# Reordered small passes of a recurrent layer: whole exponentials for the decay, keys on VectorE, memory scores between substitution steps

## The reference

```python
w = -softplus(-(w0 + tanh(dw) @ w_up)) - 0.5
a = sigmoid(a0 + da @ a_up)
kk = hs(k * k_k)                                     # 12 heads of 64
kk = kk * rsqrt(max(sum(kk * kk, -1), 1e-24))
k = hs(k * (1.0 + (a - 1.0) * k_a))
decay = exp(-exp(w))
# for each token:
sa = einsum('bhij,bhj->bhi', state, kk_t)
state = state * w_t - sa * (kk_t * a_t) + v_t * k_t
out = einsum('bhij,bhj->bhi', state, r_t)
```

## Time and profile before

| | |
|---|---|
| median of three runs | 1571.17 us |
| the profiled execution, its own time | 1572.52 us |
| its span in the trace | 1571.1 us |
| TensorE busy | 1482.2 us, 94% |
| TensorE weight load busy | 1339.4 us, 85% |
| VectorE busy | 899.7 us, 57% |
| ScalarE busy | 727.0 us, 46% |
| GpSimd busy | 96.9 us, 6% |
| mean granted TensorE clock | 0.978 of full |

### The profile page before, as it was taken

How to read it: one execution, slowest core, us unless ns; L and a number is a source line. 1 busy time by engine, 2 the same in 40 slices (tenths; PEclk the granted TensorE clock), 3 DMA queues, 4 the chain that set the end, 5 groups by cost and what they waited for, 6 DMA issues and landing times.

```text
span 1571.1 us, 23220 instructions
## 1 busy us (share of the span) xinstructions
PE 1482.2 (94%) x9817; PEld 1339.4 (85%) x9817; DVE 899.7 (57%) x1157; ACT 727.0 (46%) x1021; POOL 96.9 (6%) x122
## 2 busy tenths in 40 slices
PE   7899899999999999995999999999999998899997
PEld 5787887998789987894987899879998797789986
DVE  4765646555465556577446655566555665565554
ACT  4654544444454443875212544425444366454441
POOL 3001000000000000000211000000000112300000
PEclk9999999999999999987999999999999999999999
DMA  8634626665575663641002666547656462265651
GB/s 285 221 113 148 242 76 192 181 192 190 162 226 168 202 195 121 195 125 64 1 14 81 205 184 190 192 142 234 187 183 201 147 215 81 68 214 175 199 191 67
DMA packets 121607, 254.06 MB, mean 162 GB/s; under 512 B 8040, under 2 KB 33824, under 8 KB 121248
## 3 DMA queue, kind: packets, MB, share of 16 engines
q1 hardware_dynamic: 117200, 237.07, 48.3%
q0 software_dynamic: 4304, 15.51, 3.1%
HBM read 251.50 MB, written 1.05 MB: 161 GB/s over the span
## 4 chain that ended last, share of the span: by engine, by line
PE 81%; DVE 10%; ACT 5%; issue 2%; DMA 2%; POOL 0%; ACTq 0%; DVEq 0%; POOLq 0%
PE ps L1671 79%; DVE wl L1034 2%; DVE xres L1048 2%; DMA raw<-in_w_in 1%; ACT wh L511 1%; DVE st L1104 1%; ACT bsa L521 1%; PE ps L1763 1%; DVE xl L1042 1%; PE ps L2101 1%; PE ps L1784 0%; DVE st L1051 0%; DMA gb<-in_g_mix_pre 0%; DVE bsw L1042 0%; ACT junk L521 0%
## 5 line engine op out<-in xcount | busy, mean ns | idle before, releaser
L1034 DVE TENSOR_TENSOR wl<-raw,wh 128x1024 fp32r<-128x1024 f32 x448 | 545.6, 1226 | 471.9 <-ACT wh L511 470.0
L511 ACT ACTIVATE wh<-raw 128x1024 fp32r<-128x1024 f32 x448 | 469.8, 1058 | 481.5 <-PE ps L1671 436.9
L1671 PE MATMUL ps<-xh,wh 128*128 128x256 f32 x1792 | 505.7, 282 | 3.0 <-DVE xl L1042 3.0
L1671 PE MATMUL ps<-xl,wh 128*128 128x256 f32 x1792 | 503.1, 281 | 0.0
L1671 PE MATMUL ps<-xh,wl 128*128 128x256 f32 x1792 | 502.9, 281 | 0.0
L1671 PEld LDWEIGHTS ps<-xh,wh 128*128 128x128 f32 x1792 | 339.8, 190 | 6.1 <-DVE xl L1042 3.6
L1671 PEld LDWEIGHTS ps<-xl,wh 128*128 128x128 f32 x1792 | 339.8, 190 | 0.3
L1671 PEld LDWEIGHTS ps<-xh,wl 128*128 128x128 f32 x1792 | 339.6, 189 | 0.0
L1671 PE MATMUL ps<-wh,fhh 128*128 128x512 f32 x440 | 171.2, 389 | 0.0
L1671 PE MATMUL ps<-wl,fhh 128*128 128x512 f32 x440 | 171.2, 389 | 0.0
L1671 PE MATMUL ps<-wh,fhl 128*128 128x512 f32 x440 | 171.2, 389 | 0.0
(11 more groups left out here) (338 smaller groups left out, 1491.1 us busy)
## 6 DMA issues: line engine op xcount, KB each, us to landing
raw<-in_ffn_w_gate SPq DMA_DIRECT2D x88, 512.0 KB, 3.9
raw<-in_ffn_w_up SPq DMA_DIRECT2D x88, 512.0 KB, 4.0
raw<-in_ffn_w_down SPq DMA_DIRECT2D x88, 512.0 KB, 4.2
raw<-in_w_out SPq DMA_DIRECT2D x24, 512.0 KB, 3.5
raw<-in_w_gate SPq DMA_DIRECT2D x22, 512.0 KB, 3.8
raw<-in_w_up SPq DMA_DIRECT2D x22, 512.0 KB, 4.0
raw<-in_w_down SPq DMA_DIRECT2D x22, 512.0 KB, 4.2
raw<-in_rwkv_w_in SPq DMA_DIRECT2D x22, 512.0 KB, 4.1
```

What stands on the lines that cost most here:

```text
L511: act.activation(wh[:, i % NH, :], raw[:, i % NR, :], ACT.Copy).then_inc(act_done.new(("hi", i)), 1)
L1034: dve.tensor_tensor(wl[:, i % NH, :], raw[:, i % NR, :], wh[:, i % NH, :].bitcast(F32), ALU.subtract).then_inc(dve_done.new(("lo", i)), 1)
L1671: return pe.matmul(o, l, r, start=start, stop=stop, skip_group_check=True)
```

## The change

Five things change, all between the projection units of the recurrent layer.

1. The exponentials of the decay. Before: 12 ScalarE instructions of 128 columns for `e1` and 12 for `e3`, each with its own bias column. Now VectorE subtracts the value of token 63 from all sums in one wide subtraction (`lr`, written where the decay will stand), and ScalarE does `e3` and `e1` as one instruction each, 128x1536, in that order. Both stand behind the rounding of unit 14, and `e3` no longer stands behind the squares.
2. `kk` moves from ScalarE (six copies) to VectorE (one wide product); `kk2` writes to `LD` instead of `BV`. On VectorE `kk`, `ka`, `nb`, `kp` and `b` move ahead of `n2`, and `k1` behind it. `ze`, the small exponential, moves behind the square root `i24`.
3. `xi0`, which zeroes the off-diagonal part of the inverse, and `rk` move later; `by_row` moves ahead of `z_in(12)` and `z_in(14)` on ScalarE, and the first two gram masks on VectorE ahead of the `wl` of unit 21.
4. On VectorE the substitution steps are no longer followed by the scores: `wl` of unit 26 and `one_x(0)`, `one_x(1)` stand between step 7 and step 8. ScalarE does the exponentials of heads 0 and 1 ahead of `xi`, which stood behind it before.
5. The division by the sum is done by ScalarE (`shares`, four copies with a scale column for each pair of heads) instead of VectorE.

```diff
@@ ScalarE @@
             z_in(10, 0)
-            act.wait_ge(*dve_done.by("63"))
-            for m in range(12):
-                fn(decay[:, m, 1:P + 1], twelve(w1)[:, m, :], ACT.Exp, "e1", m, scale=DEC, bias=down63[:, m:m + 1])
-            fn(decay[:, :, 0], down63, ACT.Exp, "e0")
-            act.wait_ge(*dve_done.by("zt", 10))
-            for c in range(6):
-                copy(KK[:, c, :], Kk[:, c, :], "kk", c, scale=V("rwkv_k_k_2", c))
-            act.wait_ge(*act_done.by("kk", 5))
-            fn(BV[:, :, :], KK[:, :, :], ACT.Square, "kk2")
+            hi_to(after("rw", 0, 0))
+            act.wait_ge(*dve_done.by("zsc"))
+            fn(decay[:, :, 0], twelve(w1)[:, :, 63], ACT.Exp, "e0", scale=-DEC)
+            act.wait_ge(*act_done.by("e0"))
+            fn(twelve(w1), decay[:, :, 1:P + 1], ACT.Exp, "e3", scale=-DEC)
+            fn(decay[:, :, 1:P + 1], decay[:, :, 1:P + 1], ACT.Exp, "e1", scale=DEC)
+            act.wait_ge(*dve_done.by("kk"))
+            fn(LD, KK[:, :, :], ACT.Square, "kk2")
             hi_to(after("rw", 0, 1))
-            act.wait_ge(*act_done.by("e1", 11))
-            for m in range(12):
-                fn(twelve(w1)[:, m, :], twelve(w1)[:, m, :], ACT.Exp, "e3", m, scale=-DEC, bias=up63[:, m:m + 1])
-            fn(zsc[:, :], zsc[:, :], ACT.Exp, "ze", scale=DEC)
             hi_to(after("rw", 0, 2))
             act.wait_ge(*dve_done.by("n2"))
             fn(i24[:, :], i24[:, :], ACT.Sqrt, "i24")
+            fn(zsc[:, :], zsc[:, :], ACT.Exp, "ze", scale=DEC)
...
@@ ScalarE, after the projection @@
-            act.wait_ge(*dve_done.by("inverse_by_row"))
-            for i in range(4):
-                copy(XI[strip[i], :, strip[i]], inverse_by_row[strip[i], :].rearrange("p (m i) -> p m i", i=32)[:, 0:24, :], "xi", i)
+            def shares(h):
+                act.wait_ge(*dve_done.by("rc", "r", h))
+                for tb in range(2):
+                    copy(rpb[:, h, tb, :], rpb[:, h, tb, :], "p", "r", h, tb, scale=mem_st(h, 6)[:, tb:tb + 1])
+
             one("r", 0)
             one("r", 1)
...
+            shares(0)
+            shares(1)
+            act.wait_ge(*dve_done.by("inverse_by_row"))
+            for i in range(4):
+                copy(XI[strip[i], :, strip[i]], inverse_by_row[strip[i], :].rearrange("p (m i) -> p m i", i=32)[:, 0:24, :], "xi", i)
             one("r", 2)
             one("r", 3)
+            shares(2)
+            shares(3)
@@ VectorE @@
-            ts(down63, twelve(w1)[:, :, 63], -DEC, None, ALU.mult, ALU.bypass, "down63")
-            ts(up63, twelve(w1)[:, :, 63], DEC, None, ALU.mult, ALU.bypass, "63")
+            tt(decay[:, :, 1:P + 1], twelve(w1), twelve(w1)[:, :, 63:64].to_broadcast([P, 12, P]), ALU.subtract, "lr")
...
+            tt(KK[:, :, :], Kk[:, :, :], VB("rwkv_k_k_2"), ALU.mult, "kk")
+            lo_to(after("rw", 0, 0))
```

More of the change, by code:

```diff
@@ L830, in act_program @@
             z_in(4, 0)
[L831 to L832 removed]
+            hi_to(after("rw", 1536, 0))
             act.wait_ge(*dve_done.by("zt", 4))
@@ L835, in act_program @@
                 copy(BV[:, c, :], Rr[:, c, :], "rk", c, scale=V("rwkv_r_k_2", c))
+            hi_to(after("rw", 1536, 1))
+            act.wait_ge(*pe_done.by("norms"))
+            copy(XI, C(K_ONE, P).unsqueeze(1).to_broadcast([P, 24, P]), "xi0", scale=0.0)
+            hi_to(after("rw", 1536, 2))
+            act.wait_ge(*dve_done.by("gram", 2, 1))
+            for i in range(4):
+                copy(by_row[strip[i], 0:C7].rearrange("p (m t) -> p m t", t=32), AP[strip[i], :, strip[i]], "by_row", i)
             hi_to(after("rw", 1536, 3))
@@ L1501, in dve_program @@
                 substitute(j)
+            lo_to(after("rw", 1536, 3))
+            z_in(12)
+            z_in(14)
             lo_to(after("rw", 2048, 0))
-            for j in range(5, 10):
+            for j in range(5, 8):
                 substitute(j)
@@ L1513, in dve_program @@
             one_x(1)
+            for j in range(8, 15):
+                substitute(j)
+            one_p(0)
+            one_p(1)
+            dve.wait_ge(*dve_done.by("inverse", 14))
+            dve.transpose(inverse_by_row.rearrange("p (m i) -> p i m", i=32), inverse).then_inc(dve_done.new(("inverse_by_row",)), 1)
+            one_x(2)
+            one_x(3)
             dve.wait_ge(*dve_done.by("k1"))
```

62 lines of the change are left out of this document (20 added, 42 removed).

## The result

| | kernel before | changed kernel |
|---|---|---|
| median of 13 runs (lowest to highest) | 1570.82 us (1567.62 to 1573.98) | 1561.36 us (1555.46 to 1566.93) |
| ratio, 95% interval | | 0.9941 [0.9927, 0.9955] |
| profiled execution, span | 1572.52, 1571.1 us | 1565.0, 1563.7 us |
| mean granted clock | 0.978 | 0.983 |

The changed kernel is 9.5 us faster, by the interval 7.1 to 11.5 us. The forecast was 1563.5 us with 1560.5 to 1567.5 around it. The two profiled executions lie 7.5 us apart.

The account below looks back on a forecast made before the run. TensorE, busy 81% of the span, was taken as the bound, so only its waits in the stage counted. Gains of 1.6 and 6.1 us sum to 7.7, taking the median from 1571.2 to 1563.5 us, range 1560.5 to 1567.5.

Parts of the forecast that it names:

- Wide exponentials at 1.4 us: ScalarE, decay: each of the two wide exponentials takes 1.4 us, like the square over the same 1536 columns.
- Rival A: ScalarE, decay: the wide exponentials cost double, 2.96 us each; sum 4.9 us, time 1566.3 us; chance 0.06.
- The squares at 665.4 us: ScalarE, ahead of the norms: both wide exponentials end at 665.4 us, then the squares run until 667.0 us.
- `n2` at 674.5 us: VectorE, ahead of the norms' spreading: six wide passes and smaller work come first, giving 674.5 us against 673.8 before.
- The table load: ScalarE, at the norms: the square root's load runs ahead of its wait; a 1.28 us load follows, no drain counted.
- First term: From the sums to the spreading of the norms: a gain of 1.6 us, from -1.2 to 2.1.
- Second transpose at the same time: VectorE, at the substitution: it starts at 723.8 us as before, the earlier start being taken by 5.7 us of moved work.
- Second term: From gram to the transposes of the shares: a gain of 6.1 us, bounds 4.5 and 7.0.
- B: VectorE waits inside the substitution for the first scores; with a landing of 7.5 us, time 1567.3 us; chance with D 0.12.
- C: The substitution is held by the weight transfer; at a landing of 16 us, 4.7 us slower, 1576 us; chance 0.04.
- D: Gram to shares: scores were bound by the substitution's end, not the order; gain 2.9, time 1568.3 us; chance with B 0.12.
- The shares on ScalarE, 0.2 us: Ahead of ScalarE's copy of the first transposes: four shares, 1.65 us, mostly hidden by TensorE's transposes; 0.2 us cost.

Follow-up runs that it names:

- narrow24: The changed kernel with its two wide exponentials cut into 24 of 128 columns; median 1564.30 us, ratio 0.9959 to the kernel before.
- p1_only: The kernel before with only the edits to decay, keys and norms; gram, substitution and scores as before; median 1568.43 us, ratio 0.9988 to the kernel before.
- p2_only: The kernel before with only the edits to substitution, scores and shares; median 1564.07 us, ratio 0.9957 to the kernel before.
- xi0_late: The changed kernel with ScalarE's fill of xi0 moved behind the wait for the last gram masks, directly ahead of by_row; median 1564.37 us, ratio 0.9961 to the kernel before.
- scores_late: The changed kernel with maxima, exponentials and reciprocals of heads 0 and 1 back behind the second transpose and xi; median 1571.30 us, ratio 1.0009 to the kernel before.
- again: The changed kernel itself, unedited, run for a second trace; median 1562.25 us, ratio 0.994 to the kernel before.
- xi_late: The changed kernel with heads 2 and 3's maxima ahead of the last two substitution steps and xi's copies among the others; median 1562.81 us, ratio 0.9947 to before.
- copies_first: The changed kernel with heads 2 and 3's maxima earlier, and their shares and the first share copies ahead of xi; median 1561.95 us, ratio 0.995 to before.

## Why the prediction was right, step by step

- **Wide exponentials at 1.4 us.** Right: 3.12 us for both and `e0`. `narrow24` shows that the wide form is what the first place rests on. Rival A is out.
- **The squares at 665.4 us.** Right: 665.03. The wait for them is 1.4 us, as said (under 2).
- **`n2` at 674.5 us, against 673.8 before.** 673.7. From the end of the sums it took 16.1 us, where I had 16.4; the rest is that the whole stage began 0.5 us earlier.
- **The table load.** Right: the load for the square root was over 4 us before its operand came, and `ze` began 0.02 us behind the next load. From the decay to the rounds there are three loads before and after: the one that stood ahead of heads 0 and 1 now stands behind the square root. The Trainium skill ("ScalarE: Activation LUTs", What ACT_TABLE_LOAD costs) adds a drain of 1.38 us; this trace doesn't show one.
- **First term, 1.6 us.** The mechanism is right, the size depends on the clock. From the mark of unit 7 to gram it is 36.3 to 36.6 us in the three traces without the wide exponentials in the new order. With them it is 33.9 to 34.0 in five traces (2.4 us less than the 36.3 of before), 34.5 to 34.6 in four (1.7 to 1.8), and 35.4 in the first trace of the changed kernel (0.9). In that trace and in `p1_only` the clock from 38 to 50 us behind the start is the same, 0.86, and the spreading starts at 51.85 and 51.89; behind it the fall is deeper (0.76 over 14 us; 0.88 in `p1_only`), and that is the 1.5 us between them. I had taken 0.4 us for this. By its ratio `p1_only` gives 1.9 us, 0.2 to 3.6, but the 1.3 us of the table load are in it.
- **First transpose 5.6 us earlier.** Right: from gram 16.68 before, 11.10 after.
- **Second transpose at the same time.** 30.13 and 29.60 us from gram: 0.5 us better: the added work took 5.05 us (18.50 between the transposes instead of 13.45), where I had 5.7.
- **Exponentials of heads 2 and 3 directly behind `xi`, transposes 1.98 later.** Right: 723.77 + 3.43 = 727.20, then 727.23, then 729.22.
- **Second term, 6.1 us.** 6.2 in the first trace, 6.7 to 7.1 in the other five with this order unedited (before 51.71; 44.66 to 45.02), 6.8 by the ratio of `p2_only`. `xi0_late` shows that the start of `by_row` is passed on in full. `scores_late` shows that the moved scores are worth 3.4 us at the shares' transposes; of the 6.8 us gained there, 2.1 come without them from the earlier `by_row`, and 1.3 from the table load. `p1_only` without any edit of this place had 50.68 instead of 51.71, which is the table load less 0.3 us: that part of the term can be had from the first place.
- **Rivals B, C, D.** Out: no idle time ahead of the maxima, and `scores_late` shows that the order did bind.
- **The shares on ScalarE, 0.2 us.** Right in this order: from the shares' transposes to the rounds 7.88 us before, 8.48 in the first trace and 7.95 in `again`. `scores_late` shows that they cost a wait of 2.5 us when a reciprocal is late.
- **The sum.** 7.7 us forecast, 7.5 between the profiled executions, 9.5 between the medians. That the first two are so close is partly luck: 0.5 us of the 7.5 lie ahead of the stage, and from the start of the stage to the rounds the two traces of the changed kernel gained 7.1 and 7.4 us. The difference to the 9.5 is that of one execution from the median: 1565.0 us is the second highest of 13 runs and 3.6 us above their median, while that of before lay 1.7 us above its own. The interval, 7.1 to 11.5 us, holds the forecast. The start of the stage, with the same code ahead of it, came between 623.95 and 629.58 us in 14 traces.

What stays open: what decides where the clock falls in one execution, at the start of the stage and behind the spreading, and by what path the order of this stage lowers the clock 96 and 580 us later. And `xi_late` and `copies_first` leave the hole with a new wait each; that it can't be shorter is not shown.

## What to carry to other kernels

If two dependent chains meet at the same engines, put the small steps of the one into the list of the other, and then follow each step that changed its engine: what is queued behind it there waits with it. Judge a stage by marks on both sides of every edit, and subtract what moved ahead of the edit, before you call a trace faster. A mark at the start of the stage, 28 us ahead of the first edit, was too early here: it hid 1.1 to 1.4 us of the first place in five traces. When a small step that needs a table moves, look also at who used that table next. A gain of two or three microseconds in waits is worth only what the clock leaves of it.
